# Scores of two attention items issued tile by tile in turn

## The reference

```python
# differential: 2 maps x 4 heads of 64; 8 items
s = jnp.einsum('bqmhd,bkmhd->bmhqk', qb, k) * scale
s = s - slopes[None, None, :, None, None] * dist[:, None, None]
p = jax.nn.softmax(s, axis=-1)
a = p[:, 0] - lam * p[:, 1]
# windowed: 8 heads of 64, 2 key/value groups, a sink per head; 8 items
m = jnp.maximum(jnp.max(s, axis=-1, keepdims=True), sink_hg)
e = jnp.exp(s - m)
p = e / (jnp.sum(e, axis=-1, keepdims=True) + jnp.exp(sink_hg - m))
# MLA: 8 heads of 96; 8 items
# compressed: 8 heads of 64 against 15 blocks
s_c = jnp.einsum('bghtd,bgnd->bghtn', qblk, kc) * scale + head_bias(...)
```

## Time and profile before

| | before |
|---|---|
| median of 3 runs | 1915.56 us |
| profiled execution, its own time | 1915.18 us |
| its span, first to last instruction | 1913.3 us |
| mean granted TensorE clock | 0.942 |
| busy, share of the span | PE 95%, DVE 60%, ACT 48%, POOL 23% |
| busy on L1104 (scores of the second block) | 52.4 us |
| busy on L959 (compressed scores) | 12.4 us |

### The profile page before, as it was taken

The page is one execution under the profiler, slowest core; times in us unless marked ns, Lnnn a source line. Parts: engine busy times, 40 slices in busy tenths (PEclk is TensorE's granted clock), DMA queues, the critical chain, the costliest instruction groups (busy, mean ns, idle before and its releaser), DMA issues.

```text
span 1913.3 us, 30971 instructions
## 1 busy us (share of the span) xinstructions
PE 1813.7 (95%) x11850; PEld 1655.2 (87%) x11850; DVE 1151.3 (60%) x1608; ACT 921.1 (48%) x1571; POOL 447.4 (23%) x184
## 2 busy tenths in 40 slices
PE   7999999999999989998999999999978999999997
PEld 6899789998989789997788998999767899989995
DVE  5764464446763454446667487766555764877665
ACT  5542344445542354445554556444555555564444
POOL 2230022222330122222251022222212500222222
PEclk9985799999995789998999999999989999999999
DMA  8321145554321255553622246555545122555553
GB/s 293 139 67 56 60 169 190 183 182 169 131 78 44 77 178 191 183 184 126 217 91 89 104 133 220 186 190 193 176 144 183 69 100 91 191 187 194 186 183 115
DMA packets 80058, 284.24 MB, mean 149 GB/s; under 512 B 8847, under 2 KB 11704, under 8 KB 79416
## 3 DMA queue, kind: packets, MB, share of 16 engines
q1 hardware_dynamic: 75240, 271.16, 42.1%
q10 hardware_dynamic: 4688, 11.24, 1.7%
HBM read 281.31 MB, written 1.06 MB: 148 GB/s over the span
## 4 chain that ended last, share of the span: by engine, by line
PE 91%; DVE 5%; issue 2%; ACT 1%; DMA 0%; POOL 0%; SPq 0%; ACTq 0%; DVEq 0%
PE bank L661 42%; PE bank L675 29%; PE bank L1104 2%; PE bank L843 2%; PE bank L1131 2%; PE bank L833 2%; PE bank L895 2%; DVE w_lo L627 1%; PE bank L1112 1%; PE bank L887 1%; PE bank L796 1%; PE bank L886 1%; PE bank L702 1%; PE bank L959 1%; DVE x_t_lo L1726 1%
## 5 line engine op out<-in xcount | busy, mean ns | idle before, releaser
L627 POOL TENSOR_TENSOR w_lo<-raw,w_hi 128x1024 fp32r<-128x1024 f32 x146 | 370.7, 2539 | 1332.9 <-ACT w_hi L623 1332.7
L627 DVE TENSOR_TENSOR w_lo<-raw,w_hi 128x1024 fp32r<-128x1024 f32 x364 | 526.3, 1465 | 252.7 <-ACT w_hi L623 250.9
L623 ACT ACTIVATE w_hi<-raw 128x1024 fp32r<-128x1024 f32 x510 | 525.3, 1052 | 215.9 <-PE bank L661 131.4
L661 PE MATMUL bank<-x_t_hi,w_hi 128*128 128x256 f32 x2112 | 606.0, 287 | 4.5 <-DVE x_t_lo L1726 3.2
L661 PE MATMUL bank<-x_t_lo,w_hi 128*128 128x256 f32 x2112 | 600.4, 284 | 0.0
L661 PE MATMUL bank<-x_t_hi,w_lo 128*128 128x256 f32 x2112 | 600.2, 284 | 0.0
L661 PEld LDWEIGHTS bank<-x_t_hi,w_hi 128*128 128x128 f32 x2112 | 408.1, 193 | 11.2 <-issue 6.3
L661 PEld LDWEIGHTS bank<-x_t_lo,w_hi 128*128 128x128 f32 x2112 | 408.0, 193 | 3.1
L661 PEld LDWEIGHTS bank<-x_t_hi,w_lo 128*128 128x128 f32 x2112 | 407.9, 193 | 0.0
L675 PE MATMUL bank<-w_hi,x_t_hi 128*128 128x512 f32 (+3 forms) x384 | 135.7, 380 | 21.0 <-issue 11.6
L675 PE MATMUL bank<-w_lo,x_t_hi 128*128 128x512 f32 (+3 forms) x384 | 133.4, 374 | 0.0
(11 more groups left out here) (369 smaller groups left out, 2479.9 us busy)
## 6 DMA issues: line engine op xcount, KB each, us to landing
raw<-stream SPq DMA_DIRECT2D x511, 512.0 KB, 4.0
rows<-rows ACTq DMA_DIRECT2D x4, 1024.0 KB, 4.5
gain<-rows ACTq DMA_DIRECT2D x8, 512.0 KB, 3.7
x<-x_in SPq DMA_DIRECT2D x1, 1024.0 KB, 5.8
bias_r<-rev_dram ACTq DMA_DIRECT2D x1, 1024.0 KB, 11.2
y_out<-x SPq DMA_DIRECT2D x2, 512.0 KB, 2.7
param<-param ACTq DMA_DIRECT2D x2, 277.0 KB, 3.3
bias_r<-rev_dram ACTq DMA_DIRECT2D x1, 512.0 KB, 7.3
```

The source lines that it names most:

```text
L623: self.eng.activation(w_hi[:, i, :], raw[:, i, :], ACT.Copy).then_inc(hi_done.sem, 1)
L627: self.eng.tensor_tensor(w_lo[:, i, :], raw[:, i, :], w_hi[:, i, :].bitcast(F32), ALU.subtract).then_inc((lo_pool if self.part == "pool" e ...
L661: mm = pe.matmul(target, a[:, i, w], b[:, k0 + kt, :], start=kt + k == 0, stop=3 * kt + k == n - 1)
```

## The change

Items 0 to 15 are issued in pairs on PE, at even steps, and the tiles of the two items alternate: item i tile 0, item i+1 tile 0, item i tile 1, item i+1 tile 1. So that each pair has one head in each partition half, the windowed items take the heads in the order 0, 4, 1, 5, 2, 6, 3, 7 (slopes, sinks, values and places of the statistics follow). The bank table follows PE's new order. The compressed scores of the two groups alternate in the same way, matmul by matmul, and wait for both banks at their start.

```diff
+PAIRED = [0, 4, 1, 5, 2, 6, 3, 7]
...
     for i in range(ITEMS + 2):
-        if i < ITEMS:
+        if i < MLA and i % 2 == 0:
+            work(f"s{i}", f"s{i + 1}")
+        elif MLA <= i < ITEMS:
             work(f"s{i}")
...
-                for g in range(2):
-                    pe.wait_ge(*banks.free(at, f"cs{g}"))
-                    b = bank[banks.bank(at, f"cs{g}")]
-                    for t in range(T):
-                        for j in range(4):
-                            mm = pe.matmul(b[:, (t * 4 + j) * 16:(t * 4 + j) * 16 + 16],
...
+                for m in range(8):
+                    t, j = m // 4, m % 4
+                    for g in range(2):
+                        mm = pe.matmul(bank[banks.bank(at, f"cs{g}")][:, m * 16:m * 16 + 16],
...
+                def scores_pair(i):
...
+                    pe.wait_ge(*banks.free(at, f"s{i}"))
+                    pe.wait_ge(*banks.free(at, f"s{i + 1}"))
+                    n = i // 2 % 4
+                    for t in range(T):
+                        for half in range(2):
+                            rows_of = slice(64 * half, 64 * half + 64)
+                            if i < WIN:
+                                q, k = dq_t[rows_of, n, :], dk_t[rows_of, n, :]
+                            else:
+                                q, k = sq_t[rows_of, n, :], sk_t[rows_of, :]
+                            mm = pe.matmul(bank[banks.bank(at, f"s{i + half}")][:, t * S:(t + 1) * S],
+                                           q[:, t * P:(t + 1) * P], k, start=True, stop=True)
+                            if t == 1:
+                                mm.then_inc(*banks.fills(at, f"s{i + half}"))
...
                 for i in range(ITEMS + 3):
-                    if i < ITEMS:
+                    if i < MLA and i % 2 == 0:
+                        scores_pair(i)
+                    elif MLA <= i < ITEMS:
                         scores2(i)
```

More of the change, by code:

```diff
@@ L507, in read_p, with stat_of @@
                            ).then_inc(*banks.frees(at, f"p{i}"))
+        def stat_of(i):
+            return 2 * (WIN + PAIRED[i - WIN] if WIN <= i < MLA else i)
         PV_ENDS = {3: "od0", 7: "od1", 15: "owin", 23: "omla"}
@@ L953, in first_block @@
                 pe.wait_ge(*banks.read(at, "cmp"))
-                for g in range(2):
-                    pe.wait_ge(*banks.free(at, f"cs{g}"))
-                    b = bank[banks.bank(at, f"cs{g}")]
-                    for t in range(T):
-                        for j in range(4):
-                            mm = pe.matmul(b[:, (t * 4 + j) * 16:(t * 4 + j) * 16 + 16],
-                                           nq[64 * g:64 * g + 64, j, t * P:(t + 1) * P],
-                                           kc_t[64 * g:64 * g + 64, :], start=True, stop=True)
-                    mm.then_inc(*banks.fills(at, f"cs{g}"))
+                pe.wait_ge(*banks.free(at, "cs0"))
+                pe.wait_ge(*banks.free(at, "cs1"))
+                for m in range(8):
+                    t, j = m // 4, m % 4
+                    for g in range(2):
+                        mm = pe.matmul(bank[banks.bank(at, f"cs{g}")][:, m * 16:m * 16 + 16],
+                                       nq[64 * g:64 * g + 64, j, t * P:(t + 1) * P],
+                                       kc_t[64 * g:64 * g + 64, :], start=True, stop=True)
+                        if m == 7:
+                            mm.then_inc(*banks.fills(at, f"cs{g}"))
                 pe.wait_ge(*c["ho_squared"](at, 1))
@@ L1079, in second_block @@
                 feed(["ukv"], c_t_hi, c_t_lo, wide(0), 1, D, ["ukv0", "ukv1"], k_first=2)
-                def scores2(i):
-                    pe.wait_ge(*banks.free(at, f"s{i}"))
+                def scores_pair(i):
                     if i == 0:
@@ L1088, in scores2 @@
                         pe.wait_ge(*banks.read(at, "skt"))
[L1089 to L1101, removed]
+                    pe.wait_ge(*banks.free(at, f"s{i}"))
[12 more added lines that the diff above has]
+                                mm.then_inc(*banks.fills(at, f"s{i + half}"))
+                def scores2(i):
+                    pe.wait_ge(*banks.free(at, f"s{i}"))
+                    n, h = (i - MLA) // 2, i % 8
+                    pe.wait_ge(*banks.read(at, f"mt{n}"))
+                    pe.wait_ge(*banks.read(at, f"mt{4 + n}"))
                     b = bank[banks.bank(at, f"s{i}")]
                     for t in range(T):
-                        mm = pe.matmul(b[:, t * S:(t + 1) * S], q[:, t * P:(t + 1) * P], k, start=True, stop=True)
+                        mm = pe.matmul(b[:, t * S:(t + 1) * S], mq_t[:, h, t * P:(t + 1) * P], mk_t[:, h, :],
+                                       start=True, stop=True)
                     mm.then_inc(*banks.fills(at, f"s{i}"))
@@ L1115, in weigh2 @@
                 def weigh2(i):
-                    h = i % 8
+                    h = PAIRED[i % 8] if WIN <= i < MLA else i % 8
                     name = [n for e, n in PV_ENDS.items() if i <= e][0]
@@ L1575, in second_block @@
                             ins = act.activation(z2[:, i % 4, t * S:(t + 1) * S], source, ACT.Exp, scale=scale,
-                                                 bias=neg_max[:, 2 * i + t:2 * i + t + 1],
-                                                 accum_out=sums2[:, 2 * i + t:2 * i + t + 1])
+                                                 bias=neg_max[:, stat_of(i) + t:stat_of(i) + t + 1],
+                                                 accum_out=sums2[:, stat_of(i) + t:stat_of(i) + t + 1])
                         ins.then_inc(c["p_ready"].sem, 1)
@@ L2220, in second_block @@
                         b = bank[banks.bank(at, f"s{i}")][:]
-                        nm = neg_max[:, 2 * i:2 * i + 2]
+                        nm = neg_max[:, stat_of(i):stat_of(i) + 2]
                         dve.wait_ge(*banks.full(at, f"s{i}"))
@@ L2226, in second_block @@
                         if i < MLA:
-                            slope, table = (SLOPES[8 + i % 4], dist) if i < WIN else (SLOPES[i - WIN], dist_w)
+                            slope, table = (SLOPES[8 + i % 4], dist) if i < WIN else (SLOPES[PAIRED[i - WIN]], dist_w)
                             dve.scalar_tensor_tensor(z2[:, i % 4, :], table[:].rearrange("p t s -> p (t s)"), -slope, b,
@@ L2235, in second_block @@
                                 step(dve.tensor_reduce(nm, v, AX.X, ALU.max))
-                                dve.tensor_scalar(nm, nm, par2("sink")[:, i - WIN:i - WIN + 1], -1.0, ALU.max, ALU.mult
+                                dve.tensor_scalar(nm, nm, par2("sink")[:, PAIRED[i - WIN]:PAIRED[i - WIN] + 1], -1.0, ALU.max, ALU.mult
                                                   ).then_inc(c["z_ready"].sem, 1)
```

## The result

The changed kernel takes 1921.17 us, the median of 20 runs (1915.14 to 1930.33), against 1914.05 (1911.72 to 1920.16, 20 runs) before: ratio 1.0038, 95% interval 1.0023 to 1.0053. It is slower by 7 us. The profiled execution took 1921.04 us against 1915.18.

The account below looks back on a forecast made before the run. PE was taken to bound the kernel, holding 91% of the chain of waits; 6.2 us for waits less pairs, plus 8.7 for the clock, less 3.0 for compressed scores, added 11.9 to 1915.2: 1927 us, range 1915 to 1938.

Parts of the forecast that it names:

- Part 1, the pairs: Attention loop scores: eight pairs replace 16 items per layer, a pair saves 0.98 us, a layer 7.9 (bounds 2.6 and 9.5).
- rival 2: Attention loop pairs: the two halves overlap fully, pairs save 9.5 us a layer, kernel at 1922; chance 0.20.
- only the neighbours of different halves can overlap: Within a pair's eight score records: order A, A, B, B, A, A, B, B leaves five places of 0.215 us.
- Part 2, the banks: PE waits for DVE to free score banks, mainly steps 8, 10, 13: new 12.9 us, old 1.9, 11.0 more a layer.
- The rotation's 0.3: PE's wait for DVE's rotation in the attention loop, claimed to fall from 1.24 us to some 0.3.
- the 3.1 of my sum: Attention layer: 11.0 us more waiting less 7.9 saved by pairs makes it 3.1 us longer, two layers 6.2.
- Part 3, the clock: PE at half clock after three long waits: 5.1 us a layer, 10.2 in all, less 1.5 already paid: 8.7.
- Part 4, the compressed scores: 32 records taking 6.12 us a layer: alternating halves saves 1.5 us, two layers 3.0 (full overlap 3.1 a layer).
- The signs of it: Changed profile: pairs about 1.3 us, gate unit waits 4.4, 2.5, 3.4, transpose 1.4, PEclk 0.50 behind each, 32 records in 4.6.
- rival 1: Attention loop pairs: no overlap at all, pairs save only the height changes, 2.6 us a layer, kernel at 1938; chance 0.13.

Follow-up runs that it names:

- item-by-item run: The changed kernel, but within a pair both tiles of the first item go before both of the second (A, A, B, B): 1925.43 us, ratio 1.0058.
- run with filled waits: The changed kernel, with PE repeating the last item's weighing 4, 3 and 4 times ahead of gate units 8, 10 and 13: 1912.93 us, ratio 1.0000.

## Why the prediction was right, and what was mis-sized

I predicted 1927 us, in a range of 1915 to 1938, and slower by more than 0.3%; it is 1921.2, slower by 0.38%, with an interval (0.23 to 0.53%) that reaches below 0.3. The direction and its cause hold; the size was 12 us and is 7.

- **Part 1, the pairs: the wrong value between the bounds.** I took 1.40 a pair (five places of 0.215) and it is 1.19, full overlap, which was rival 2. It is also the Trainium skill's rule on row groups (TensorE: Matmul & The Clock Gate, "The mechanism"), and the trace agrees with it: the first two records of the pair at 964.96 start within 0.01 us of each other. The step that failed is "only the neighbours of different halves can overlap". The item-by-item run shows that program order within the pair doesn't matter. 16 pairs of 0.21 are 3.4 us.
- **Part 2, the banks: right, wait for wait.** Expected 1.4, 4.4, 2.5 and 3.4; measured 1.09, 4.09, 2.51 and 3.32. (For gate unit 8, 5.0 less 0.43 gives 4.6 and not the 4.4 that I wrote.) The rotation's 0.3 was 0.52. The runs in which DVE reads at once, or in which the three pairs are undone, take these waits away and the loss with them. With the clock held up, the layer is 3.1 us longer than before, which is the 3.1 of my sum, but that is luck, by two errors that cancel: the pairs saved 1.6 more, and the waits cost about as much more. All waits together were as I had them, 13.1 us idle for my 12.9, with one of 0.38 on ACT among them that I had not listed. What my sum put at nothing is that a wait costs more than its idle time: the two steps with one wait of 0.53 take 10.42 us (975.18 to 985.60), 0.81 more than the two without. Some 0.25 for each of eight waits, where there were two before, is the missing 1.5 (an estimate from these rows).
- **Part 3, the clock: right in kind, a little too dear.** I charged 10.2 us for both layers. Against the run with filled waits the layers lost 4.8 and 3.7 (95.5 against 91.8), 8.5 in all, since the clock stayed up behind the wait of 2.5. Less the 1.5 that the execution before had paid, 7.0 in place of 8.7. The waits are the same in both layers and their price is not, so it is no fixed figure for a wait.
- **Part 4, the compressed scores: undersized.** 5.2 us on PE in place of 3.0; alone they bring 4.4 at the medians and 5.2 in the trace. The fuller bound of 3.1 a layer was close (2.6).
- *The signs of it.* The profile was to show pairs of 1.3 us, waits at gate units 8, 10 and 13, half clock behind each, and 4.6 us for the compressed scores. The second came as written, the third for two of three, the first and last were better than written.
- *A slip in rival 1.* 12.9 less 0.9 is 12.0 and not 11.7, so its 1938 should be 1939. It changes neither the forecast nor the account.

By these terms: 6.2 - 3.4 + about 3 for what waits cost beyond their idle time + 7.0 - 5.2 is 7.6 us, near the 7.1 measured.

The range of one kernel's runs is wide here, and the clock goes with it: among the change's 20 runs, the mean granted clock is 0.944 in those of 1915 us and 0.933 in those of 1930. At which waits those executions differ no trace shows, since one execution of each kernel was profiled.

## What to carry to other kernels

When two results are made side by side, look at who empties their buffers, and in which order its program comes to the second one: a buffer is wanted back by rotation, not by need, and a reader that does other work between the two turns a saving of 1.2 us into waits of 2.5 to 4.1. Change the reader's order with the writer's; here that turned a loss of 7 us into a gain of 18, and of 24 with one unit moved over a known wait. And price idle TensorE at more than its length: here 8.5 us of clock came on top of the waits. The length of a single wait doesn't tell whether it will: half clock followed waits of 4.1 and 3.3 us and not those of 2.5, but it also followed one of 2.34 and, in both layers of one version, three of 0.5, 1.1 and 0.9 us close together. Read the granted clock behind each.

## What the hardware showed that I had not expected

- Two fp32 matmuls over opposite partition halves run wholly beside each other, also when each half has two in a row: eight records took 1.06 us in one order and 1.07 in the other, four took 1.06 before.
- Matmuls of 16 columns gain too, though not by half: from 0.19 us a record to 0.11, at clock 0.50. Their weight loads, each a record of 0.33 us, close up with them: 22 in 3.9 us before, 32 in 3.5 us now.
- Idle PE can cost more than repeated work: 11 repeated weighings a layer made the kernel 7 to 8 us faster, with the clock at 1.00 where it had been at 0.50.
